# An encoder layer on one core: the row scale earlier, the attention scores of two items side by side, and exponentials before outputs

## The reference

```python
h = rmsnorm(x, norm_mix)
z = h @ w_in                       # 1024 x 3072: q, k, v, b_g, c_g, xc of 512 columns each
q, k = rmsnorm per head of 64      # 8 maps: 4 heads, two maps each
for each head and block of 128 queries:
    s = q k^T / 8 + bias(relative position)        # bias: 32 buckets x 8 maps
    p = softmax(s)
    a = p[map 0] - lam * p[map 1]
    o = a @ v
o_att = rmsnorm(o) * 0.8
o_conv = b_g * conv3(c_g * xc)     # width 3 over positions, per channel
x = x + concat(o_att, o_conv) @ w_out
x = x + moe(rmsnorm(x))            # 16 experts, best group, best two experts in it
x = x + sigmoid(x @ w_g) * rmsnorm(p @ w_p)
```

## Time and profile before

| | |
|---|---|
| median of 3 runs | 607.11 us (607.06 to 607.49) |
| the profiled execution, its own time | 605.1 us |
| its span, first to last instruction | 603.3 us |
| PE busy | 595.0 us (99%) |
| DVE, ACT, POOL busy | 419.5, 329.3, 68.8 us |
| granted TensorE clock | 1.00 throughout |

### The profile page before, as it was taken

One profiled execution on the slowest core, in us unless ns is written; L12 is line 12 of the kernel. 1 busy time (PEld: TensorE's weight loads), 2 busy tenths in 40 slices (PEclk: granted clock), 3 DMA queues, 4 the chain that ended last, 5 costly groups with the idle time before them and its releaser, 6 DMA issues.

```text
span 603.3 us, 8730 instructions
## 1 busy us (share of the span) xinstructions
PE 595.0 (99%) x3160; PEld 490.7 (81%) x3160; DVE 419.5 (70%) x781; ACT 329.3 (55%) x595; POOL 68.8 (11%) x109
## 2 busy tenths in 40 slices
PE   9999999999999999999999999999999999999997
PEld 6888989888887787888877887778888888878886
DVE  5522993354552566746878789899999999688863
ACT  6851030222232676656556566789999998961211
POOL 0250000000000000100100113242221220210000
PEclk9999999999999999999999999999999999999999
DMA  8945827120212412213324677999999999775611
GB/s 330 373 71 189 315 105 273 36 74 31 77 63 71 183 36 105 71 70 106 106 72 143 249 255 257 389 371 415 411 410 410 413 411 374 290 297 205 221 47 65
DMA packets 39042, 126.52 MB, mean 210 GB/s; under 512 B 6448, under 2 KB 7472, under 8 KB 38968
## 3 DMA queue, kind: packets, MB, share of 16 engines
q1 hardware_dynamic: 33224, 112.97, 51.1%
q0 software_dynamic: 4896, 12.59, 5.4%
q10 hardware_dynamic: 880, 0.41, 0.2%
HBM read 113.33 MB, written 23.10 MB: 226 GB/s over the span
## 4 chain that ended last, share of the span: by engine, by line
PE 80%; DMA 8%; DVE 6%; POOL 2%; issue 1%; ACT 1%; SPq 1%; ACTq 0%; DVEq 0%; POOLq 0%
PE bank L508 19%; PE bank L510 18%; PE bank L509 18%; PE bank L1929 7%; PE bank L1946 3%; PE bank L1965 3%; PE bank L538 3%; PE bank L540 3%; PE bank L539 3%; DMA x_T<-in_xT 2%; DMA row_scale<-x_rstd 2%; POOL bias_sb L801 2%; PE bank L2240 1%; PE bank L2080 1%; DMA pick<-moe_rows 1%
## 5 line engine op out<-in xcount | busy, mean ns | idle before, releaser
L503 DVE TENSOR_TENSOR w_split<-w_raw,w_split 128x1024 fp32r<-128x1024 f32 x33 | 40.5, 1229 | 21.8 <-ACT w_split L498 21.6
L508 PE MATMUL bank<-w_split,moe_xT 128*128 128x512 f32 x120 | 48.5, 404 | 0.8 <-DVE w_split L1700 0.8
L510 PE MATMUL bank<-w_split,moe_xT 128*128 128x512 f32 x120 | 47.0, 392 | 0.0
L509 PE MATMUL bank<-w_split,moe_xT 128*128 128x512 f32 x120 | 46.8, 390 | 0.0
L1018 ACT ACTIVATE sq_tmp<-bank 128x512 f32<-128x512 f32 x12 | 7.2, 598 | 69.7 <-PE bank L510 69.7
L498 ACT ACTIVATE w_split<-w_raw 128x1024 fp32r<-128x1024 f32 x33 | 34.5, 1051 | 19.1 <-DMA w_raw<-in_w_in 18.8
L985 ACT ACTIVATE s<-s,mn 128x512 f32<-128x512 f32 (+1 forms) x48 | 30.9, 645 | 18.7 <-DVE mn L1436 18.7
L508 PE MATMUL bank<-w_split,x3T 128*128 128x512 f32 (+1 forms) x104 | 39.4, 379 | 0.5 <-DVE x3T L1878 0.5
L487 DVE TENSOR_TENSOR w_split<-w_raw_more,w_split 128x1024 fp32r<-128x1024 f32 x32 | 38.0, 1217 | 2.7 <-ACT w_split L481 2.7
L510 PE MATMUL bank<-w_split,x3T 128*128 128x512 f32 (+1 forms) x104 | 38.9, 374 | 0.0
L509 PE MATMUL bank<-w_split,x3T 128*128 128x512 f32 (+1 forms) x104 | 38.8, 373 | 0.0
(11 more groups left out here) (321 smaller groups left out, 1594.6 us busy)
## 6 DMA issues: line engine op xcount, KB each, us to landing
w_raw<-in_w_moe SPq DMA_DIRECT2D x32, 512.0 KB, 15.0
w_raw_room<-in_w_moe SPq DMA_DIRECT2D x30, 512.0 KB, 16.0
w_raw_more<-in_w_moe SPq DMA_DIRECT2D x30, 512.0 KB, 16.4
w_raw<-in_w_in SPq DMA_DIRECT2D x23, 512.0 KB, 9.4
pick<-moe_rows SPq DMA_DIRECT2D x12, 512.0 KB, 5.0
bias_rows<-bias_table SPq DMA_DIRECT2D x1, 4096.0 KB
w_raw<-in_w_out SPq DMA_DIRECT2D x8, 512.0 KB, 3.4
toep<-bias_rows SPq DMA_DIRECT2D x4, 896.0 KB, 7.0
```

The source lines that it names most:

```text
L503: nc.vector.tensor_tensor(W[:, u % WS, 1], raw(u)[0], f(W[:, u % WS, 0]), ALU.subtract).then_inc(lo_done, 1)
L508: nc.tensor.matmul(out, hi, whi, start=first, stop=False)
L509: nc.tensor.matmul(out, lo, whi, start=False, stop=False)
L510: return nc.tensor.matmul(out, hi, wlo, start=False, stop=last)
```

## The change

**Row scale.** GpSimd waits for the squares and makes the scale first, and fills the bias table after it. SP stores the scale and loads it back at weight unit 8, at once; the table is stored at unit 13 and spread at unit 15 (before: at units 8 and 10). The scale has a semaphore of its own. ScalarE's wait for the scale moves from ahead of the first block's copies to the first use, at q. VectorE's first product of the gate waits only for the table's store.

**Scores.** PE issues `scores(1)` and `scores(2)` in the last projection of v, and then `scores(w)` and `scores(w+1)` in each odd step w from 3; the even steps have none.

**Other work.** Of the twelve matmuls of an output half in an odd step, the last three move to the head of the next, even step. An odd step has six and three matmuls, an even step nine and six. Steps 1 to 4 keep six and six.

**Exponentials.** In the even steps from 8 to 22 ScalarE has `exps(w)` ahead of `o_out(w-2)`; before, behind it.

```diff
--- before.py
+++ after.py
@@ -349,6 +349,7 @@
         a_sq, d_ss, a_sd = sem("act_qk_square"), sem("dve_qk_sum"), sem("act_qk_std")
         a_lam = sem("act_lambda_exp")
         rs_ld, a_b, b_st = sem("row_scale_loaded"), sem("act_row_scale2"), sem("bias_stored")
+        sc_st = sem("row_scale_stored")
         toep_ld = [sem(f"toep_loaded{i}") for i in range(HEADS)]
         pe_s, d_s, a_e, d_a = (sem(n) for n in (
             "pe_scores", "dve_scores", "act_exp", "dve_a"))
@@ -606,23 +607,25 @@
                 unit(w_in[u] if u < OUT0 else w_out[u - OUT0], u)
                 if u == 8:
 
-                    sp.wait_ge(g_sum, 1 + len(RUNS))
-                    sp.dma_start(bias_dram, bias_sb[:]).then_inc(b_st, 16)
                     sp.wait_ge(g_xr, 2)
                     with nc.allow_non_contiguous_dma(reason="one value of a token"):
-                        sp.dma_start(scale_dram.rearrange("i p -> p i"), x_rstd[:]).then_inc(b_st, 16)
-                if u == 10:
-                    sp.wait_ge(b_st, 32)
+                        sp.dma_start(scale_dram.rearrange("i p -> p i"), x_rstd[:]).then_inc(sc_st, 16)
+                    sp.wait_ge(sc_st, 16)
                     for q in range(2):
                         sp.dma_start(rs[q][:], bass.AP(scale_dram.tensor, q * SEQS[0], [[0, P], [1, SEQS[q]]])
                                      ).then_inc(rs_ld, 16)
+                if u == 13:
+                    sp.wait_ge(g_sum, 2 + len(RUNS))
+                    sp.dma_start(bias_dram, bias_sb[:]).then_inc(b_st, 16)
+                if u == 15:
+                    sp.wait_ge(b_st, 16)
                     sp.dma_start(bias_rows, bass.AP(bias_dram.tensor, 0, [[REL, MAPS], [0, P], [1, REL]])
                                  ).then_inc(b_st, 16)
                 if u == 20:
                     sp.dma_start(cl[:], late).then_inc(late_ld, 16)
                     for j in range(2):
                         sp.dma_start(y_dram[j * TOK:j * TOK + P], zeros).then_inc(late_ld, 16)
-                    sp.wait_ge(b_st, 48)
+                    sp.wait_ge(b_st, 32)
                     sp.wait_ge(a_xq, TILES)
                     toeplitz(0)
             sp.wait_ge(pe_acc, TILES * V_B + VP)
@@ -796,22 +799,23 @@
         def _(pool):
             pool.memset(mhalf[:], -0.5).then_inc(g_sum, 1)
             pool.wait_ge(g_sum, 1)
+            steps = [1]
+
+            def inv_root(ss, n, e):
+
+                steps[0] += 1
+                pool.tensor_scalar(ss, ss, e, None, ALU.add).then_inc(g_sum, 1)
+                pool.wait_ge(g_sum, steps[0])
+                return pool.tensor_tensor(ss, ss, mhalf[:, 0:n], ALU.pow)
+
+            pool.wait_ge(a_xq, TILES)
+            pool.tensor_scalar(x_veps[:], x_rstd[:], EPS, EPS, ALU.add, ALU.mult).then_inc(g_xr, 1)
+            inv_root(x_rstd[:], TILES, EPS).then_inc(g_xr, 1)
             pool.wait_ge(c_ld, 16 * 6)
             for k, c0, c1 in RUNS:
                 pool.tensor_scalar(bias_sb[:, c0:c1], relb[:, k:k + 1].broadcast_to([MAPS, c1 - c0]),
                                    -1.0, None, ALU.mult).then_inc(g_sum, 1)
-            steps = [1 + len(RUNS)]
-
-            def inv_root(ss, n, e):
-
-                steps[0] += 1
-                pool.tensor_scalar(ss, ss, e, None, ALU.add).then_inc(g_sum, 1)
-                pool.wait_ge(g_sum, steps[0])
-                return pool.tensor_tensor(ss, ss, mhalf[:, 0:n], ALU.pow)
-
-            pool.wait_ge(a_xq, TILES)
-            pool.tensor_scalar(x_veps[:], x_rstd[:], EPS, EPS, ALU.add, ALU.mult).then_inc(g_xr, 1)
-            inv_root(x_rstd[:], TILES, EPS).then_inc(g_xr, 1)
+            steps[0] += len(RUNS)
 
             def o_std(i):
                 ss = o_ssq[:, HEADS * i:HEADS * (i + 1)]
@@ -974,7 +978,6 @@
                 x_square(i)
             split_hi(6)
             split_hi(7)
-            act.wait_ge(g_xr, 2)
 
             def exps(w):
 
@@ -1012,6 +1015,8 @@
                             act.activation(rs2[q][:], rs[q][:], ACT.Square).then_inc(a_b, 1)
                     elif b in (Q_B, K_B):
                         r = n - TILES * Q_B
+                        if r == 0:
+                            act.wait_ge(g_xr, 2)
                         act.wait_ge(pe_acc, n + 1)
                         if r >= 1:
                             act.wait_ge(d_ss, r)
@@ -1093,6 +1098,8 @@
                 for half in range(2):
                     if w - 1 - half in H2_AT:
                         x2T_out(H2_AT[w - 1 - half], half)
+                if w >= 8 and w % 2 == 0 and w < NI:
+                    exps(w)
                 if w >= 2:
                     o_out(w - 2)
                 if w in LATE_UNITS:
@@ -1101,7 +1108,7 @@
                 if w == 4:
                     act.wait_ge(lo_done, OUT0 + 5)
                     split_conv_hi(0)
-                if 2 <= w < NI:
+                if 2 <= w < NI and (w < 8 or w % 2):
                     exps(w)
                 evac_aT(w - 1)
                 if w == 1:
@@ -1399,7 +1406,7 @@
                 cs, ts, sample = span(i)
                 dve.wait_ge(pe_acc, n + 1)
                 if i == 0:
-                    dve.wait_ge(b_st, 48)
+                    dve.wait_ge(b_st, 16)
                 if sample:
                     out = gcs[:, 4:6, 1, cs].rearrange("p t c n -> p c t n")
                     a, b_ = (bank[n % 3][:].rearrange("p (c t n) -> p c t n", c=2, t=2),
@@ -2053,11 +2060,13 @@
                         pe.wait_ge(acc_free[(n - 1) % 3], (n - 1) // 3 + 1)
                         turn(out, src, 4, pe_t)
 
-                    if b == V_B and i % 2:
-                        if i == 1:
-                            for m in range(TJ[Q_B] + 2, TJ[K_B] + TILES):
-                                t_ready(pe, m)
-                        scores(i // 2)
+                    if b == V_B and i == 1:
+                        for m in range(TJ[Q_B] + 2, TJ[K_B] + TILES):
+                            t_ready(pe, m)
+                        scores(0)
+                    elif b == V_B and i == 3:
+                        scores(1)
+                        scores(2)
 
             def turn_o(i):
                 pe.wait_ge(d_on, i + 1)
@@ -2095,16 +2104,23 @@
                 if w in V_AT:
                     project(V_B, VP + part, (2 * V_AT[w], 2 * V_AT[w] + 1))
                 elif w in CONV_AT:
-                    conv_part(*CONV_AT[w], range(2 * part, 2 * part + 2))
+                    i, half = CONV_AT[w]
+                    if half and not part:
+                        conv_part(i, 0, range(3, 4))
+                    conv_part(i, half, range(2 * part, 4 if half and part else 2 + part))
                 elif w in ATT_AT:
-                    att_part(*ATT_AT[w], range(4 + 2 * part, 6 + 2 * part))
+                    i, half = ATT_AT[w]
+                    if half and not part:
+                        att_part(i, 0, range(7, 8))
+                    att_part(i, half, range(4 + 2 * part, 8 if half and part else 6 + part))
 
             for w in range(1, NI + 1):
                 if w == 5:
                     for n in range(34, 36):
                         pe.wait_ge(acc_free[n % 3], n // 3 + 1)
-                if 2 <= w < NI:
-                    scores(w)
+                if w >= 3 and w % 2:
+                    for j in range(w, min(w + 2, NI)):
+                        scores(j)
                 chunk(w, 0)
                 if w - 1 in O_AT:
                     pe.wait_ge(d_mix, O_AT[w - 1] + 1)
```

More of the change, by code:

```diff
@@ L798, in _ @@
             pool.wait_ge(g_sum, 1)
-            pool.wait_ge(c_ld, 16 * 6)
-            for k, c0, c1 in RUNS:
-                pool.tensor_scalar(bias_sb[:, c0:c1], relb[:, k:k + 1].broadcast_to([MAPS, c1 - c0]),
-                                   -1.0, None, ALU.mult).then_inc(g_sum, 1)
-            steps = [1 + len(RUNS)]
+            steps = [1]
             def inv_root(ss, n, e):
@@ L814, in _ @@
             inv_root(x_rstd[:], TILES, EPS).then_inc(g_xr, 1)
+            pool.wait_ge(c_ld, 16 * 6)
+            for k, c0, c1 in RUNS:
+                pool.tensor_scalar(bias_sb[:, c0:c1], relb[:, k:k + 1].broadcast_to([MAPS, c1 - c0]),
+                                   -1.0, None, ALU.mult).then_inc(g_sum, 1)
+            steps[0] += len(RUNS)
             def o_std(i):
```

## The result

The changed kernel takes 609.11 us (median of 22 runs, 607.62 to 610.46), the kernel before 607.09 in the same comparison (605.08 to 610.30). The ratio is 1.0033, with a 95% interval of 1.0018 to 1.0047: slower by 1.1 to 2.9 us. The forecast was 610.1, slower. The profiled execution of the changed kernel took 608.15 with a span of 606.3, against 605.1 and 603.3: +3.05, where the sum said +3.0. The agreement is better than its parts, and that the medians give +2.0 where the profiled executions give +3.05 is itself a finding.

What follows compares the result with a forecast made beforehand. PE, busy 595.0 of 603.3 us at full clock, bounds the kernel; -1.17 - 4.4 - 0.57 + 6.8 + 1.0 + 1.15 + 0.25 gave +3.0 (rounded): 608.1 profiled, 610.1 median. Own range 608.2 to 611.5, whole 603.8 to 612.3.

Steps and rivals of the forecast that it cites:

- The start: First blocks: the earlier row scale removes PE's gaps at 40 and 57 us, -1.17 us.
- Fewer entries: Attention loop: pairing cuts groups of scores on PE from 24 to 13, 0.40 saved each, -4.4 us.
- `mix_lo`: Step 7: PE's 0.5 wait for `mix_lo(0)` goes behind a second group of scores, -0.57 us with the slow first matmul.
- Rival C: Loop: the switch from `pv` to split matmuls also costs 0.40 at each of 11; +5.2, 612.3 us; chance 0.10.
- Even steps: Steps 8 to 22: `pv` waits for the transposed item's copy, which stands behind exponentials on ScalarE, +6.8 us.
- The two steps counted from `turn_o`: Steps 10 and 14: `pv` waits 1.08 us each for the copy, due at T + 4.35, started at T + 5.43.
- Step 8: Counted from `turn_a(6)`: copy ready at U + 7.01, PE at U + 6.18, so `pv` waits 0.83 us.
- The four of the sample: Steps 16 to 22, even ones: wait taken as 0.85 us each, nearest to step 8, 3.4 in all.
- the output's place: Even steps: `o_out` now behind the exponentials delays the copy by 0.6 us each, 4.6 of the 6.8.
- Odd steps: Steps 5 to 15, six with 512 keys: `pv` waits 0.16 us each for the copy, +1.0 us.
- steps 2 to 5: Later `turn_a(0)` delays the chain, 0.7 in step 2, 0.25 in step 4; step 5's scores wait 0.2; +1.15 us.
- The turns: Steps 16, 20 and 24: `turn_a` comes a little ahead of `combine` and waits, +0.25 us more than before.

Runs made afterwards that it cites:

- e2: Kernel before with only the row scale's earlier chain, without pairing, moved products or exponentials moved ahead; 603.89 us, ratio 0.9955.
- e4: Changed kernel without the moved products, six and six matmuls in every step; 611.67 us, ratio 1.0085 to the kernel before.
- e5: Kernel before plus 32 extra score-like matmuls in two projections of v, in sixteen groups between split matmuls; 621.97 us, ratio 1.0239.
- e6: Kernel before plus 32 extra score-like matmuls in one group directly before the scores of item 1; 613.24 us, ratio 1.0108.
- e1: Changed kernel with ScalarE's exponentials behind the outputs again in even steps; 603.78 us, ratio 0.9951 to the kernel before.
- e8: e1 plus the copy ahead of exponentials in even steps from 2, three and six matmuls in odd steps, combination ahead of VectorE's convolution split; 599.46 us, ratio 0.9880.

## Why the prediction was right, point by point

**The start (-1.17): under-sized for the medians.** In the profiled execution it brought 1.30 (189.57 to 188.27). In the medians it brought 2.7 (e2), and the other kernels bear this out: taking what each loop costs from the difference of its medians leaves 1.7 us for the start in e4 and 2.1 to 3.0 in the rest. My term was made against one execution, whose first scores were the earliest of the five with the old start. The forecast of 610.1 carried the 2.0 between the profile of before and its median over to the changed kernel. That step was wrong: most of this distance goes with the old start. For the changed kernel the +2.0 of the medians is +4.8 in the loop and -2.8 in the start, where I had +4.2 and -1.2. So the start made the forecast 1.6 too high and the loop 0.6 too low, 1.0 together.

**Fewer entries (-4.4): right.** 0.416 each (e5, e6), 4.6 in all. `pv` to split matmuls is free: the four places start 0.03 after `pv`'s last matmul, as those behind transposes. Rival C falls.

**`mix_lo` (-0.57): right.** The row is gone. Before, PE's scores of step 7 started 1.64 ahead of the next matmul, and those of the prompt's other items 1.06 or 1.07; in the changed kernel the pair of step 7 takes 1.93, as the prompt's other pairs do.

**Even steps (+6.8): the mechanism right, the size 1.1 too large.** 0.70, 1.06, 0.26, 1.06, 0.66, 0.63, 0.65, 0.67 sum to 5.69. The two steps counted from `turn_o` were met to 0.02. Step 8 measured 0.70 for 0.83, step 12 0.26 for 0.4. The four of the sample, which I took by the nearest step at 0.85, measured 0.65: 0.8 of the error. The share of the output's place, 4.6, is what e1 gave back (4.54).

**Odd steps (+1.0) and steps 2 to 5 (+1.15):** 0.95, and 0.72 + 0.17 + 0.12 (the scores of step 5, which start 1.21 behind `pv` and not 1.09): 1.0. The turns waited 0.31 more, against 0.25, and the matmuls behind them started 0.14 later in themselves.

**What was missing: +1.9.** A `pv` that waited costs 0.10 more in itself; in e1 even one that waited 0.02 us does. In the rows above its record is 1.16 long against 1.06 in the earlier trace rows: the second half of its first matmul starts 0.21 behind the first and not 0.11, and all later ones keep 0.11. That happens in 16 steps of the changed kernel, and with 0.04 to 0.05 in the four odd ones of the sample from 17 on, where no wait shows at all. The groups of the two kernels by line (busy us, mean ns, idle before) carry it, 21.7 before, 23.6 after:

```profile
L1965 PE MATMUL bank<-v_tok,a_T 128*128 128x128 f32 x160 | 21.7, 274 | 0.0
L1972 PE MATMUL bank<-v_tok,a_T 128*128 128x128 f32 x160 | 23.6, 286 | 4.9 <-ACT a_T L1047 4.8
L1972 PEld LDWEIGHTS bank<-v_tok,a_T 128*128 128x128 f32 x160 | 19.9, 191 | 13.1 <-ACT a_T L1047 12.8
```

The last row points at the reason: the copy is the weight of these products, and the load of weights (PEld), which otherwise runs beside the matmuls, waits 12.8 us for it in all, where PE itself is listed with 4.8. My reading is that a copy that is in time by less than the load needs costs PE something without a wait being listed. No run separates this from another cause. That the extra goes when the copies come early is shown: in e8 the group is back at 21.8.

**The sum of the loop** was to be +4.2 (3.0 without the start's -1.17) and is +4.82: -4.6 - 0.6 + 5.7 + 0.95 + 1.0 + 1.9 + 0.45 makes 4.8. Behind the loop 0.5 came back, within what executions differ there. The forecast's +3.0 was thus met in the trace by errors of opposite sign, and that is luck: waits of the even steps 1.1 too long, 1.9 of `pv` itself unseen, 0.5 back behind the loop. What was right without luck is the order of the terms: pairing pays 4.6, the output's place takes 4.6 away, and what the scores' absence uncovers takes the rest. Pairing and moved products by themselves are worth nothing here (e1 against e2: 142.61 and 142.30 us of loop); they pay once the copy leaves its place behind the exponentials (e8).

**Open.** The 22 runs of the changed kernel scatter over 2.8 us and those of e4 over 3.0, while e1, with the same start, stays within 0.3. The granted clock of each run tells part of it: nine of the 22 have 0.996 or 0.997 and take 609.37 to 610.46; the other thirteen have 0.999 or 1.0 and take 607.62 to 609.24, but for one of 609.88. In e4 the three longest of six have 0.996 or 0.997. So PE stood at its lower level for a time in these runs. Both kernels have waits of 1 us and more in the loop that e1 does not have, but no profiled execution of either has the lower level there (0.999), so where it falls is not shown.

## What to carry to other kernels

On an engine with a fixed order, put ahead of a wait what is ready before it, and above all what the bounding engine waits for: here the copy (for `pv`) ahead of the exponentials, which nobody needs until the next step. When work is taken out between two dependent steps of the bounding engine, list the chain on the other engines that it had covered and shorten it in the same edit. And build a forecast of a median on more than one execution where the profile has a gap that hangs on a DMA or on GpSimd. To tell edits of a few tenths apart, cut out the stretch between two fixed rows: here it repeated to 0.05 us over five executions, where the medians of the kernel before lay between 605.6 and 607.1.

## What the runs showed of the hardware

- A group of 64-row matmuls between 128-row ones costs 0.416 us beyond its work, once per group, of one pair or of sixteen (e5, e6).
- A `pv` whose weights arrived just in time or late was 0.10 us longer in itself: 0.21 between its first two starts, and not 0.11 (changed kernel, e1).
- After a pause of PE of 2.45 us the granted clock stood at 0.59 over the next 4 us (e6), after one of 1.97 at 0.71 over 3 us (e5, 81 to 84); after one of 1.28 (e5, at 57 us) it stayed full. Over the longest runs of the kernel before it was 0.994.
- GpSimd's 31 small instructions for the table took 10.4 to 10.5 us in five executions and 11.3 in e6, and 8.5 to 8.6 in the eight in which they began behind the scale.
